# PEER retrieval on Trainium2: one-hots on three engines, five dots of sixteen on TensorE, eight V slots

## What is computed

```python
s1, s2 = scores of q against two sets of 128 subkeys     # top 16 of each, then top 16 of 256 sums
idx  = i1 * 128 + i2                                      # (token, 128 picks)
gate = softmax(best_s)
act  = gelu(einsum('td,tkd->tk', h, peer_u[idx]))         # U rows: dot products
out  = einsum('tk,tkd->td', act * gate, peer_v[idx])      # V rows: weighted sum
h    = layer_norm(alpha * h + gt2 * out)
```

## Time and profile before

| | us |
|---|---|
| median of 3 runs | 3490.19 |
| lowest and highest | 3486.7 and 3492.4 |
| profiled execution, its own time | 3493.18 |
| span of its core in the profile | 3491.5 |
| U loop ends at | 2904.7 |
| V sum begins on TensorE at | 2966.4 |
| V sum ends on TensorE at | 3406.2 |

### The profile page before, as it was taken

The page is one execution under the profiler, slowest core; times in us unless marked ns, Lnnn a source line. Parts: engine busy times, 40 slices in busy tenths (PEclk is TensorE's granted clock), DMA queues, the critical chain, the costliest instruction groups (busy, mean ns, idle before and its releaser), DMA issues. The chain is left out here.

```text
span 3491.5 us, 35993 instructions
## 1 busy us (share of the span) xinstructions
PE 3175.9 (91%) x12602; PEld 2031.3 (58%) x12602; DVE 2136.3 (61%) x3994; ACT 635.7 (18%) x1127; POOL 996.9 (29%) x618
## 2 busy tenths in 40 slices
PE   7999999999999999999999999887677768999990
PEld 2456667575757666777544444666666766444440
DVE  6543444444434444665756425888899988666667
ACT  2312212121212122111000011233233424000000
POOL 0011102020211113000000011455644462876773
PEclk8999999999999999999999999998888889999995
DMA  9754454545364544554554597999998893999996
GB/s 359 291 219 181 181 200 166 216 152 224 129 234 154 209 183 182 202 186 174 206 180 169 211 334 281 384 374 377 394 385 337 318 396 152 394 419 420 419 419 245
DMA packets 171354, 930.26 MB, mean 266 GB/s; under 512 B 19736, under 2 KB 32857, under 8 KB 89305
## 3 DMA queue, kind: packets, MB, share of 16 engines
q1 hardware_dynamic: 85386, 494.13, 38.0%
q0 software_dynamic: 73728, 402.69, 28.9%
q10 hardware_dynamic: 12112, 31.79, 2.3%
HBM read 907.29 MB, written 21.23 MB: 266 GB/s over the span
## 5 line engine op out<-in xcount | busy, mean ns | idle before, releaser
L1078 PE MATMUL ps<-mT,ring 128*128 128x256 f32 (+1 forms) x4096 | 1168.9, 446 | 1.1 <-PEq L215 1.1
L1078 PEld LDWEIGHTS ps<-mT,ring 128*128 128x128 f32 x4096 | 774.9, 190 | 388.1 <-issue 318.3
L2156 POOL DMA_INDIRECT u_rows<-in_peer_u_dram,expert_indices x172 | 267.9, 1558 | 283.9 <-DVE dots L2453 117.0
L2453 DVE CUSTOM_DVE_ANT_0 u_rows<-u_rows,yhy 128x2048 f32<-128x2048 f32 x130 | 293.8, 2287 | 57.8 <-DMA u_rows<-in_peer_u_dram,expert_indices 44.6
L2669 PE MATMUL ps<-mT,turned_rows 128*128 128x128 f32 x2016 | 301.0, 304 | 22.3 <-ACT turned_rows L2230 20.7
L2669 PEld LDWEIGHTS ps<-mT,turned_rows 128*128 128x128 f32 x2016 | 279.1, 216 | 38.0 <-issue 38.0
L710 POOL TENSOR_TENSOR dd<-mask_f,dt_g 128x1024 f32<-128x1024 f32 x16 | 30.4, 1897 | 933.1 <-DVE dt_g L980 932.4
L2165 POOL DMA_INDIRECT scores<-in_v_rest_dram,expert_indices x140 | 203.1, 1451 | 136.0 <-DVE turned_rows L2495 56.2
L870 DVE SCALAR_TENSOR_TENSOR conv<-ps,tap_g,conv 128x510 f32<-128x510 f32 (+1 forms) x48 | 33.8, 704 | 338.7 <-ACT conv L731 338.7
L2498 DVE SCALAR_TENSOR_TENSOR turned_rows<-scores,expert_gate,turned_rows 128x1024 f32<-128x1024 f32 x138 | 176.9, 1286 | 96.8 <-DMA scores<-in_v_rest_dram,expert_indices 95.8
L2230 ACT COPY turned_rows<-ps 128x512 f32<-128x512 f32 x252 | 144.1, 586 | 439.7 <-PE ps L2661 433.6
(11 more groups left out here) (392 smaller groups left out, 4475.2 us busy)
## 6 DMA issues: line engine op xcount, KB each, us to landing
ring<-in_w_stream_dram SPq DMA_DIRECT2D x160, 1024.0 KB, 4.9
ada_tiles<-in_w_ada_dram SPq DMA_DIRECT2D x64, 1024.0 KB, 6.7
yhy<-in_v_dense_dram SPq DMA_DIRECT2D x128, 512.0 KB
ring<-in_w_mix_dram SPq DMA_DIRECT2D x48, 1024.0 KB, 4.8
ring<-in_w_mod_dram SPq DMA_DIRECT2D x32, 1024.0 KB, 10.5
ring<-in_w_out_dram SPq DMA_DIRECT2D x32, 1024.0 KB, 7.3
rows<-cum_rows_scratch SPq DMA_DIRECT2D x16, 1536.0 KB, 13.0
ring<-in_w_q_dram SPq DMA_DIRECT2D x12, 1024.0 KB, 9.4
```

Source lines behind the costliest of these rows:

```text
L1078: mm = nc.tensor.matmul(ps[:, k % 4, 0:n], m.ring[:, slot, kt * P:(kt + 1) * P], m.mT[:, kt, 0:n], start=(kt == 0), stop=(kt == KT - 1))
L2156: nc.gpsimd.indirect_dma_start(u_slot[j % NU], None, d.peer_u, bass.IndirectOffsetOnAxis(ap=eidx[:, j:j + 1], axis=0)).then_inc(u_in[j % N ...
L2453: nc.vector.tensor_tensor_reduce(out=u_slot[j % NU], in0=u_slot[j % NU], in1=h2[:, t, :], scale=1.0, scalar=0.0, op0=ALU.mult, op1=ALU.add ...
```

## The change

- One-hots are made four tokens at a time, as 128x512, in two buffers. In the first tile the vector engine makes the i1 part with one comparison; GpSimd makes the squared distances of the i2 part with a subtraction and a product; the scalar engine turns them into ones and zeros by relu(1 - d) and scales the i1 part. In the second tile the vector engine makes both parts, and GpSimd scales.
- The groups of the first tile stand in slots 36 to 63 of the loop, one in each and two in slots 40, 44, 48 and 52.
- TensorE takes five rows of sixteen (2, 5, 8, 11, 14 of a unit) in place of four, the vector engine eleven.
- V rows keep eight slots to the end. The last 16 rows are eight of the first tile, then eight of the second. `h` comes back into `u_rows` once half of the dense tiles are summed, and with it the gate and norm rows, into `gate_rows`.
- The finishing of the dense columns stands between V rows 235 and 244, and the first tile is finished, normalised and stored while the second is still being added.

```diff
         acc = turned_rows[:].rearrange("p a b -> p (a b)").rearrange("p (t n) -> p t n", n=HALF_D)
-        gt2 = keys[:].rearrange("p a b -> p (a b)")
-        lng2, lnb2 = scores_rows[:, 0:D], scores_rows[:, D:2 * D]
+        gt2 = gate_rows[:, 0, :]
+        gated = keys[:].rearrange("p (r a) b -> p r (a b)", r=4)
+        lng2, lnb2 = gate_rows[:, 1, :], gate_rows[:, 2, :]
+        h_last = m.u_rows[:, 0:TT, :]
 
         mods_in = sem("e_scale_shift_rows_loaded")
         small = sem("f_small_loaded")
...
-        def on_pe(j):
-            return j % 4 == 3 and j // 4 < N_PE
+        BY_PE = (2, 5, 8, 11, 14)
+        PE_ROWS = [j for j in range(ROWS) if j % TOPK in BY_PE]
+        N_PE = len(PE_ROWS)
+
+        def pe_rows(j):
+
+            return sum(i <= j for i in PE_ROWS)
 
         def dve_rows(j):
 
...
         def v_pair(k):
 
-            return PAIRS_OF * (k % TT) + k // TT
-
-        FIRST_SPREAD, LAST_SPREAD = (9, 0), (12, 3)
-
-        def spread_at(u, h):
-
-            k = 4 * (u - FIRST_SPREAD[0]) + h
-            return range(2 * k, 2 * k + 2) if FIRST_SPREAD <= (u, h) <= LAST_SPREAD else ()
+            m = k - (ROWS - 2 * V_LAST)
+            if m < 0:
+                return PAIRS_OF * (k % TT) + k // TT
+            return PAIRS_OF * (m // V_LAST) + PAIRS_OF - V_LAST + m % V_LAST
+
+        FIRST_SPREAD, DOUBLE = NB * PH + 4, (40, 44, 48, 52)
+
+        def spread_at(s):
+
+            if not FIRST_SPREAD <= s < NB * UNITS:
+                return range(0)
+            first = s - FIRST_SPREAD + sum(d < s for d in DOUBLE)
+            return range(first, first + (2 if s in DOUBLE else 1))
 
...
+                def squared_distances(n):
+                    pool.wait_ge(pair_a, 1)
+                    if n >= 2:
+                        pool.wait_ge(spread_p, n - 1)
+                    far = one_hot[:, n % 2, 1]
+                    nc.gpsimd.tensor_tensor(far, iota[:].unsqueeze(1).to_broadcast([P, 4, NKEY]),
+                                            by_pair[:, 2, 4 * n:4 * n + 4].unsqueeze(2).to_broadcast([P, 4, NKEY]), ALU.subtract).then_inc(hot_p, 1)
+                    pool.wait_ge(hot_p, 2 * n + 1)
+                    nc.gpsimd.tensor_tensor(far, far, far, ALU.mult).then_inc(hot_p, 1)
+
+                def scale_one_hots(n):
+                    k = n + P // 4
+                    pool.wait_ge(hot_v, P // 4 + 2 * n + 1)
+                    nc.gpsimd.tensor_tensor(one_hot[:, k % 2, 0], one_hot[:, k % 2, 0],
+                                            by_pair[:, 0, 4 * n:4 * n + 4].unsqueeze(2).to_broadcast([P, 4, NKEY]), ALU.mult).then_inc(hot_p, 1)
+
+                hots_before = {}
+                for s in range(FIRST_SPREAD, NB * UNITS):
+                    for i, n in enumerate(spread_at(s)):
+                        hots_before.setdefault(4 * s + 4 + 2 * i, []).append(n)
                 for j in range(ROWS):
+                    for n in hots_before.get(j, ()):
+                        squared_distances(n)
                     if j % TOPK == 0:
                         pool.wait_ge(idx_v, j // TOPK + 1)
...
+                for n in hots_before.get(ROWS, ()):
+                    squared_distances(n)
                 for k in range(ROWS):
                     if k == 4:
...
+                    if k == NV:
+                        for n in range(P // 4):
+                            scale_one_hots(n)
+                    if k >= NV:
+                        pool.wait_ge(acc_v, k - NV + 1)
                     pool.sem_inc(pool_step, 1)
                     nc.gpsimd.indirect_dma_start(
-                        v_slot[v_at(k)], None, d.v_rest, bass.IndirectOffsetOnAxis(ap=eidx[:, v_pair(k):v_pair(k) + 1], axis=0)).then_inc(v_in[v_at(k)], 16)
+                        v_slot[k % NV], None, d.v_rest, bass.IndirectOffsetOnAxis(ap=eidx[:, v_pair(k):v_pair(k) + 1], axis=0)).then_inc(v_in[k % NV], 16)
 
...
+                def finish_one_hots(n):
+
+                    act.wait_ge(hot_p, 2 * n + 2)
+                    near = one_hot[:, n % 2, 1]
+                    nc.scalar.activation(near, near, ACT.Relu, bias=1.0, scale=-1.0).then_inc(hot_a, 1)
+                    act.wait_ge(hot_v, n + 1)
+                    for a in range(4):
+                        token = 4 * n + a
+                        nc.scalar.activation(one_hot[:, n % 2, 0, a, :], one_hot[:, n % 2, 0, a, :], ACT.Copy,
+                                             scale=by_pair[:, 0, token:token + 1]).then_inc(hot_a, 1)
...
                 def one_hots(t, n):
 
+                    k = n + t * P // 4
                     v.wait_ge(pair_a, t + 1)
-                    done = n + t * P // 4
-                    if done >= 2:
-                        v.wait_ge(spread_p, done - 1)
-                    for a in range(4):
-                        token = 4 * n + a
-                        s = 2 * (token % 8)
-                        nc.vector.tensor_scalar(one_hot[:, s, :], iota[:], by_pair[:, 1, token:token + 1], by_pair[:, 0, token:token + 1],
-                                                ALU.is_equal, ALU.mult)
-                        nc.vector.tensor_scalar(one_hot[:, s + 1, :], iota[:], by_pair[:, 2, token:token + 1], None,
-                                                ALU.is_equal).then_inc(hot_v, 1)
+                    if k >= 2:
+                        v.wait_ge(spread_p, k - 1)
+                    for r in range(1 + t):
+                        nc.vector.tensor_tensor(one_hot[:, k % 2, r], iota[:].unsqueeze(1).to_broadcast([P, 4, NKEY]),
+                                                by_pair[:, 1 + r, 4 * n:4 * n + 4].unsqueeze(2).to_broadcast([P, 4, NKEY]), ALU.is_equal).then_inc(hot_v, 1)
 
...
-                act.wait_ge(acc_v, ROWS)
-                spread(lng2, d.ln[2], ln2_in)
-                spread(lnb2, d.ln[3], ln2_in)
-                root(rstd[:], var[:])
+                                  src.rearrange("(o a) n -> o (a n)", o=1).unsqueeze(0).to_broadcast([P, 1, D])).then_inc(last_in, 16)
+
+                act.wait_ge(vt_used, HALF)
+                act.dma_start(h_last, d.h_rows).then_inc(last_in, 16)
+                spread(gt2, d.mod_rows[3 * KT:4 * KT])
+                spread(lng2, d.ln[2])
+                spread(lnb2, d.ln[3])
+                for t in range(TT):
+                    root(rstd[:, t:t + 1], var[:, t:t + 1])
 
             @block.vector
...
                 def add_row(k):
 
-                    t, first = k % TT, k < TT
-                    _, landed = v_before(k)
+                    t = v_pair(k) // PAIRS_OF
                     coefficient = gate[:, v_pair(k):v_pair(k) + 1]
-                    v.wait_ge(v_in[v_at(k)], landed)
-                    if first:
-                        nc.vector.tensor_scalar(acc[:, t, :], v_slot[v_at(k)], coefficient, None, ALU.mult).then_inc(acc_v, 1)
+                    v.wait_ge(v_in[k % NV], 16 * (k // NV) + 16)
+                    if k < TT:
+                        nc.vector.tensor_scalar(acc[:, t, :], v_slot[k % NV], coefficient, None, ALU.mult).then_inc(acc_v, 1)
                     else:
-                        v.wait_ge(acc_v, k - 1)
-                        nc.vector.scalar_tensor_tensor(acc[:, t, :], v_slot[v_at(k)], coefficient, acc[:, t, :],
+                        v.wait_ge(acc_v, k - 1 if k <= ROWS - 2 * V_LAST else k)
+                        nc.vector.scalar_tensor_tensor(acc[:, t, :], v_slot[k % NV], coefficient, acc[:, t, :],
                                                        ALU.mult, ALU.add).then_inc(acc_v, 1)
 
...
+                def finish_early_columns(t, k):
+                    cols = slice(k * CH, (k + 1) * CH)
+                    v.wait_ge(last_in, 64)
+                    v.wait_ge(ffn_pe, 2 * t + k + 1)
+                    n = c.inc(nc.vector.tensor_tensor(gated[:, 2 * t + k, :], gt2[:, cols], ps[:, 2 * t + k, :], ALU.mult))
                     v.wait_ge(st, n)
-                    for t in range(TT):
-                        n = c.inc(nc.vector.scalar_tensor_tensor(m.h[:, t, HALF_D:D], m.h[:, t, HALF_D:D], ALPHA, acc[:, t, :], ALU.mult, ALU.add))
+                    n = c.inc(nc.vector.scalar_tensor_tensor(h_last[:, t, cols], h_last[:, t, cols], ALPHA, gated[:, 2 * t + k, :], ALU.mult, ALU.add))
                     v.wait_ge(st, n)
-                    for t in range(TT):
-                        for k in range(2, 4):
-                            n = c.inc(nc.vector.bn_stats(stats[:, t, k, :], m.h[:, t, k * CH:(k + 1) * CH]))
+                    c.inc(nc.vector.bn_stats(stats[:, t, k, :], h_last[:, t, cols]))
+
...
                 for k in range(ROWS):
                     add_row(k)
-                finish_late_columns()
-                finish_early_columns()
+                    if k in EARLY_AT:
+                        finish_early_columns(*EARLY_AT[k])
+                    if k == ROWS - V_LAST - 1:
+                        finish_late_columns(0)
```

(17 more changed lines are left out.)

134 lines of the change are left out of this document (61 added, 73 removed).

## The result

The change makes the kernel slower. After it the median is 3543.14 us (four runs, 3530.49 to 3546.91), the kernel before took 3489.32 us beside it: a ratio of 1.0148, 95% interval 1.012 to 1.0175. The forecast was 3502 us with a range of 3460 to 3538. The sign was right (slower had 0.55), the size was not, and the time lies past the range. For each experiment the median is given, and behind it the ratio to the kernel before, run beside it, with its 95% interval. One execution each of experiments 4 and 15 took far longer (6315.54 and 5553.47 us, at a lower granted clock) and is left out of their medians and ratios.

What follows compares the result with a forecast made beforehand. Transfers were taken to pace the bare U loop, the vector engine the one-hots, transfers with a never-idle TensorE the V sum. Terms -8 + 5 + 20 - 5 = +12 us gave 3502 us beside the median, range 3460 to 3538.

Steps and rivals of the forecast that it cites:

- The sign: Whole kernel: slower had 0.55, with +12 us in total; the second one-hot stretch's term alone was said to carry it.
- Five rows on TensorE: U loop: a fifth TensorE row costs +4 us in each of two units with query projections; sum +5, bounds -4 and +16.
- The late units: Units 9 to 14, first-tile one-hots: 278 us against 289.5; with the loop's end -8 us, bounds -31 and +33.
- the queue: GpSimd's queue in slots 40, 44, 48, 52: gathers stand behind a wait; 2.5 us each, 10 us.
- The lock's price: First-tile one-hots: GpSimd operations hold back vector dots, 1.3 us a group, bounds 0 and 2.3; nothing where the vector engine ranks.
- The end of the loop: End of the U loop: row 254 on TensorE takes about 8 us where a dot takes 2.2; 3 us later.
- One-hots of the second tile: Between U loop and V sum: comparisons and GpSimd's product exclude each other, 78 us; +20 us, bounds -15 and +25.
- V sum and end: After the one-hots: 83.2 us from TensorE's end to the span's end, against 88.1; -5 us, bounds -15 and +2.
- The rivals: Pool operations hide: 3479 us (0.20); full lock price: 3532 (0.17); no lock: 3444 (0.08); end gives more: 3492 (0.10).
- Rival 2: U loop: GpSimd's lock costs its full price, 49.3 us a unit; +42 us, 3532 us; chance 0.17.

Runs made afterwards that it cites:

- experiment 4: Changed kernel with four rows of 16 on TensorE, at 2, 5, 8, 14: 3534.36 us, ratio 1.0132.
- 15: Changed kernel without GpSimd one-hot work, five TensorE rows only from unit 9, spaced loads, queries sooner on vector and scalar engines: 3461.45 us, ratio 0.9917.
- Experiment 7: Kernel before with the five TensorE rows, and the vector and scalar engines' parts of the queries moved sooner: 3514.16 us, ratio 1.0063.
- experiment 3: Changed kernel with five rows of 16 on TensorE at 3, 7, 9, 11, 15: 3539.34 us, ratio 1.0135.
- Experiment 8: Changed kernel with TensorE rows 3, 7, 11, 15 up to unit 8 and its five rows from unit 9: 3505.34 us, ratio 1.004.
- experiment 9: Changed kernel with TensorE rows 3, 7, 11, 15 and GpSimd's one-hot operations replaced by memsets that read nothing: 3478.08 us, single run.
- Experiments 1: Kernel before with only the five TensorE rows (2, 5, 8, 11, 14) changed: 3531.30 us, ratio 1.0121.
- 11: Changed kernel without GpSimd one-hot work, TensorE rows 3, 7, 11, 15 before unit 9 and its five rows from there: 3461.94 us, ratio 0.9921.
- experiment 2: Changed kernel with four rows of 16 on TensorE, at 3, 7, 11, 15, without row 255: 3523.85 us, ratio 1.0103.
- experiment 13: Changed kernel with TensorE rows 3, 7, 11, 15, no GpSimd one-hot work, and V-stretch loads 16 dense tiles apart: 3473.29 us, ratio 0.9953.
- Experiment 12: Kernel before with only the V part changed: eight slots, loads at half of the dense tiles, end tile by tile: 3490.19 us, ratio 0.9998.
- experiment 10: Changed kernel with TensorE rows 3, 7, 11, 15 and one-hots on vector and scalar engines, none on GpSimd: 3476.33 us, ratio 0.9952.

## Why the prediction was wrong, step by step

**Five rows on TensorE: +5, measured +28. This is the step that failed.** It said "+4 us in each of the two such units, nothing in the others", and it came from TensorE's load: 6.5 us a row against an engine busy 43.3 of 46 us. Units 1 and 3 grew by 5.9 and 7.4 us, and the other seven, put at nothing, by 14 together. Experiment 7 shows that load is worth 6 us over units 0 to 5 (8 us over units 0 to 8), close to what was priced; in experiment 3, with other places, it is up to 12 to 15. What was left out is the order: rows 5 and 8 stand on either side of a step that three engines do in turn, where row 7 stood at its edge. The step's waits were in the trace of before, 11.5 us in 3, and I did not ask what would be queued behind them with other rows. "The slot of a row is free sooner than its product", counted as a small gain, is true only when TensorE is free to turn it. In the profiles the whole change is 37 us where 12 were put, and 23 of these 25 us are this term's. The profiled execution lies inside the forecast's range; the median left it by the 11 to 16 us of the other executions, which no trace shows.

**The late units: 278 forecast, 285.3 measured,** inside the term's bounds. That is 47.6 us a unit where 46.3 was put (44.6 and 1.7 for the queue). Experiment 8, with the same code there, took 294.9, so the gain of 4.2 us is no more than one execution's. The lock's price was close, its place was not. Over the 21 groups between 2599 and 2803 us the dots lost (2583 - 2287) x 32 + (2518 - 2286) x 16 ns = 13 us. Four kinds of small instruction, which I took as free of it, lost nearly as much: `expert_gate` 6.4 us in place of 1.1, the cast of `rank_f` 3.7 for 0.7, the copy of `scores` 3.6 for 1.1, `softmax_arg` 2.9 for 1.1, together 12.6 us. With 3.4 us on the comparisons that is 1.4 us a group against the 1.3 of the sum, but "nothing where the vector engine ranks" was wrong. These are lengthened instructions; what GpSimd's own time ahead of the gathers costs beside them is not separated. The Trainium skill (SBUF — State Buffer, Who interferes with whom) says that copy, cast and tensor_scalar can enter a mode that takes both ports and so contend with GpSimd; the trace agrees. It also says that a GpSimd instruction that only writes does not hold up a two-input one; experiment 9's dots at 2287 ns agree. In the forecast I used only the half of that section on two inputs.

**The end of the loop: +3 forecast, +7.5 measured,** and for another reason. It was put down to row 254 on TensorE. Experiments 1 and 11 have that row there and end in 58.3 and 59.5 us, less than the 60.5 of before; experiment 2 has it not and needs 66.7, and loses 5 of them with memsets (61.9). So it goes with GpSimd's operations, some 5 us of the 8 with the form that reads.

**One-hots of the second tile: +20 forecast, +10 measured.** The mechanism was right: comparisons that took 0.61 us take 0.9 beside the product, and memsets bring the stretch to 57 us. The size was not. The timeline of the kernel after, one group in 2.05 us:

```profile
2950.84 1.42 POOL L2168 TENSOR_TENSOR keys<-keys,by_pair 128x512 f32<-128x512 f32 x1 [0.63 <-DVE keys L2525]
2951.55 1.86 DVE L2525 TENSOR_TENSOR keys<-iota,by_pair 128x512 f32<-128x512 f32 x2 [0.19 <-PE ps L2766]
...
2952.89 1.42 POOL L2168 TENSOR_TENSOR keys<-keys,by_pair 128x512 f32<-128x512 f32 x1 [0.63 <-DVE keys L2525]
2953.59 1.86 DVE L2525 TENSOR_TENSOR keys<-iota,by_pair 128x512 f32<-128x512 f32 x2 [0.19 <-PE ps L2766]
```

Two comparisons alone would take 1.2 us; the period leaves some 0.85 for the product, where 1.15 and "a little" were put. The rows fit three operations that take turns: the comparisons end at 2953.41 us (2951.55 + 1.86), the product that began at 2952.89 ends at 2954.31, which leaves it 0.90 us to itself. Its record of 1.42 us is longer than the time that it adds.

**V sum and end: -5 forecast, -5.3 measured, by two errors that cancel.** "While TensorE works" its sum was taken as fixed; it grew by 10.5 us (439.2 to 449.7), of which TensorE waits 6.2 for dense tiles; in experiment 13, with the loads spaced, the sum took 440.5. Behind it 83 us were forecast and 70.1 measured. Experiment 12 gives this part alone as 0 (-4 to +2 us), so the -5.3 of the profile may not be all its own.

**The rivals.** None of the four came in. Rival 2, the full price of the lock, gave 3532 us and so lies nearest, but for the wrong cause: its units of 49.3 us measured 47.6. The sign rests on more than the five rows: the other terms add up to +8.2 us in the profiles, where +7 was put. That agreement is luck, since the loop's end and late units came out 11 us worse and the second one-hots 10 us better. Experiment 8, the change without the early loss, lies 16 us above the kernel before.

## What to carry to other kernels

When work is moved to another place in an in-order engine's program, list the waits of that engine in the same slots and ask what will now be queued behind them; a wait that costs nothing with one neighbour can cost some 6 us with the next (17 us over three such waits in experiment 4). Read such a step on all the engines that take part in it: moving it on one of them moved the wait, and only moving it on the vector and the scalar engine together paid. And an operation given to GpSimd beside a busy vector engine is priced by what it holds up, small copies and casts too, and by the gathers that queue behind it; doing it on the busy engine may be cheaper, as it was in experiment 10.

## What the hardware showed that was not expected

- A 128x16 tensor_scalar, 0.28 us by itself, took 1.60 us on average beside GpSimd's tensor_tensors and 2.24 us beside its memsets; the max and find_index instructions of the ranking kept their length to 1 ns (283 and 285 ns before and after).
- The two-input dots lost 0.3 us on average beside GpSimd's reads, up to 1.5 us each (3808 ns), and nothing beside its writes (2287 ns).
- GpSimd's 128x512 product recorded 1.42 us beside the comparisons and stretched their period by some 0.85 us.
